# Layer embedding: the rounding of p, the splits of the first gate slabs, and the squares of the last gate slab, moved in the ScalarE and VectorE programs

## What is computed

```
f = swiglu_2(rmsnorm_2(h, g[4]), ffn_gate[i, 1], ffn_up[i, 1], ffn_down[i, 1])
h = h + MACARON * rmsnorm_2(f, g[5])
gate = jax.nn.sigmoid(rmsnorm_2(h, g[6]) @ w_ple_gate[i])
h = h + rmsnorm_2((p[i].astype(h.dtype) @ w_ple[i]) * gate, g[7])
```

## Time and profile before

| | us |
|---|---|
| median of 3 runs (1806.93 to 1814.6) | 1810.8 |
| the profiled execution itself | 1805.07 |
| its span, first to last instruction | 1803.4 |
| TensorE busy | 1713.6 (95%) |
| VectorE busy | 1180.2 (65%) |
| ScalarE busy | 897.7 (50%) |

### The profile page before, as it was taken

The page is one execution under the profiler, slowest core; times in us unless marked ns, Lnnn a source line. Parts: engine busy times, 40 slices in busy tenths (PEclk is TensorE's granted clock), DMA queues, the critical chain, the costliest instruction groups (busy, mean ns, idle before and its releaser), DMA issues.

```text
span 1803.4 us, 30032 instructions
## 1 busy us (share of the span) xinstructions
PE 1713.6 (95%) x11890; PEld 1595.1 (88%) x11890; DVE 1180.2 (65%) x1492; ACT 897.7 (50%) x1238; POOL 109.2 (6%) x161
## 2 busy tenths in 40 slices
PE   7988999999999999999999999988999998999996
PEld 4987999998899989999898899978999898899986
DVE  7988889867774456555675655565655675665556
ACT  4576533466543445343575543455433567543445
POOL 2110211100010000000020000000000003000000
PEclk9998999999999999999998999998999999999998
DMA  9983799946465554555441455534555442355550
GB/s 382 333 318 140 272 381 362 361 148 246 158 217 189 185 189 147 188 185 186 143 173 44 163 194 195 185 130 140 201 184 187 174 143 92 112 204 186 178 194 36
DMA packets 61924, 353.80 MB, mean 196 GB/s; under 512 B 6522, under 2 KB 9738, under 8 KB 27792
## 3 DMA queue, kind: packets, MB, share of 16 engines
q1 hardware_dynamic: 40064, 281.24, 42.6%
q0 software_dynamic: 18384, 66.66, 10.1%
q10 hardware_dynamic: 3392, 4.72, 0.8%
HBM read 349.45 MB, written 3.15 MB: 196 GB/s over the span
## 4 chain that ended last, share of the span: by engine, by line
PE 81%; DVE 9%; ACT 5%; issue 3%; DMA 2%; POOL 1%; DVEq 0%; ACTq 0%; POOLq 0%
PE bank L499 24%; PE bank L500 24%; PE bank L501 24%; DVE w_lo L1540 2%; ACT w_hi L1019 2%; PE bank L531 1%; PE bank L533 1%; PE bank L532 1%; PE bank L674 1%; DVE shared L2109 1%; DVE shared L1562 1%; DMA shared<-in_mods 1%; DVE x L2118 1%; DVE work L1924 1%; PE bank L557 1%
## 5 line engine op out<-in xcount | busy, mean ns | idle before, releaser
L499 PE MATMUL bank<-a_hi,w_hi 128*128 128x256 f32 x2648 | 757.2, 286 | 13.5 <-DVE a_lo L1613 3.8
L501 PE MATMUL bank<-a_hi,w_lo 128*128 128x256 f32 x2648 | 753.4, 285 | 0.0
L500 PE MATMUL bank<-a_lo,w_hi 128*128 128x256 f32 x2648 | 753.3, 284 | 0.0
L499 PEld LDWEIGHTS bank<-a_hi,w_hi 128*128 128x128 f32 x2648 | 512.4, 194 | 19.9 <-issue 10.4
L500 PEld LDWEIGHTS bank<-a_lo,w_hi 128*128 128x128 f32 x2648 | 512.4, 194 | 2.7 <-issue 0.5
L501 PEld LDWEIGHTS bank<-a_hi,w_lo 128*128 128x128 f32 x2648 | 512.0, 193 | 0.0
L1807 DVE TENSOR_TENSOR w_lo<-raw,w_hi 128x2048 fp32r<-128x2048 f32 x144 | 330.1, 2292 | 246.2 <-ACT w_hi L1160 246.2
L1160 ACT CAST w_hi<-raw 128x2048 fp32r<-128x2048 f32 x144 | 274.0, 1904 | 270.2 <-PE bank L501 270.2
L1540 DVE TENSOR_TENSOR w_lo<-raw,w_hi 128x2048 fp32r<-128x2048 f32 x122 | 279.5, 2294 | 135.9 <-ACT w_hi L1019 135.7
L1019 ACT CAST w_hi<-raw 128x2048 fp32r<-128x2048 f32 x122 | 231.6, 1907 | 90.8 <-PE bank L501 84.1
L499 PE MATMUL bank<-w_hi,hid_hi 128*128 128x512 f32 x548 | 216.2, 395 | 3.9 <-DVE hid_lo L2283 3.1
(11 more groups left out here) (251 smaller groups left out, 1904.3 us busy)
## 6 DMA issues: line engine op xcount, KB each, us to landing
raw<-in_stream SPq DMA_DIRECT2D x266, 1024.0 KB, 4.8
shared<-in_mods POOLq DMA_DIRECT2D x104, 512.0 KB, 6.8
grow<-in_rows POOLq DMA_DIRECT2D x12, 512.0 KB, 4.0
work<-in_mods POOLq DMA_DIRECT2D x8, 512.0 KB, 9.6
bias_rows<-work ACTq DMA_DIRECT2D x1, 2048.0 KB, 23.2
x<-in_x_t SPq DMA_DIRECT2D x1, 1024.0 KB, 6.0
x<-in_x_d ACTq DMA_DIRECT2D x1, 1024.0 KB, 7.6
work<-bias_rows ACTq DMA_DIRECT2D x1, 1024.0 KB, 8.6
```

Of the source, the lines that this page charges most:

```text
L499: pe.matmul(out, w_h, v_h, start=start, stop=False, skip_group_check=True)
L500: pe.matmul(out, w_h, v_l, start=False, stop=False, skip_group_check=True)
L501: return pe.matmul(out, w_l, v_h, start=False, stop=stop, skip_group_check=True)
```

## The change

Four moves, made for both layers of the second block. No instruction is added or removed, and TensorE's program is the same.

- ScalarE rounds p when the product of slab b+31 is done (`slab_done` at b+32), not b+32 (`slab_done` at b+33). Half 1 of `hid_hi` is last read by slab b+31.
- ScalarE rounds gate slabs b+34 and b+35 behind the roots of `post`. Before, one stood ahead of p and one between p and `post`.
- VectorE takes the low part of b+34 behind `post`. Before, it stood ahead of p.
- At the fourth gate slab ScalarE sums the squares ahead of the rounding of the next slab, not behind it. In layer 1 there is no next slab.

```diff
-            def ffn(i, b):
+            def ffn(i, b, embedded=None):
...
                 hidden_hi(j, j % 2, b + 3 * j - 1)
-                split_to(b + 3 * j + 5)
+                if embedded is not None:
+
+                    act.wait_ge(slab_done, b + 3 * FJ - 1)
+                    act.copy(hid_hi[:, 1], ptok[:, embedded]).then_inc(ph_ready, 1)
+                else:
+                    split_to(b + 3 * j + 5)
...
-                ffn(3 + 2 * l, bf)
-                act.wait_ge(slab_done, bf + 3 * FJ)
-                act.copy(hid_hi[:, 1], ptok[:, l]).then_inc(ph_ready, 1)
-                split_to(bf + 3 * FJ + 3)
+                ffn(3 + 2 * l, bf, l)
                 u = u2(l, 2)
                 post(u, 6 + 3 * l, bf + 3 * FJ - 1)
+                split_to(bf + 3 * FJ + 3)
                 turned_hi(u, gain2(l, 6))
...
-                    if i == 3:
+                    if i < 3:
+                        split_to(base2(l, M_PGATE) + i + 3)
+                        gated_squares(i)
+                    else:
                         warm_up()
-                    split_to(base2(l, M_PGATE) + i + 3)
-                    gated_squares(i)
+                        gated_squares(i)
+                        split_to(base2(l, M_PGATE) + i + 3)
...
         @block.vector
-                split_to(b + 3 * j + 5)
+                if i < 2 or i % 2 == 0:
+                    split_to(b + 3 * j + 5)
...
                 dve.tensor_tensor(hid_lo[:, 1], ptok[:, l], hid_hi[:, 1].bitcast(F32), ALU.subtract).then_inc(pl_ready, 1)
+                post(u2(l, 2), 6 + 3 * l, bf + 3 * FJ - 1, 0.5)
                 split_to(bf + 3 * FJ + 2)
-                post(u2(l, 2), 6 + 3 * l, bf + 3 * FJ - 1, 0.5)
```

## The result

| | median, us | runs | ratio to before, 95% interval |
|---|---|---|---|
| before | 1808.87 | 4 | |
| changed | 1789.46 (1788.47 to 1791.92) | 4 | 0.9894 [0.9873, 0.9916] |

The change saves 19.4 us (1.1%), between 15 and 23 by the interval. The forecast was 17.8 saved and 1793.0. The profiled execution took 1790.37, its span is 1788.7.

A forecast was written before the change was run, and what follows sets the result against it. The start of ScalarE's squares was taken to bound the stretch ahead of each layer's gate slabs. Twice 8.0 plus 1.8 gave 17.8 us, 1810.8 to 1793.0; likeliest range 1791 to 1797, with the first two rivals 1785 to 1802.

The forecast's parts named there:

- What bounds the stretch: Between the second network's last down product and the gate slabs, the start of ScalarE's squares sets the 15.8 us.
- The squares and the end of the residual: At each layer's second residual, the first square moves from 1195.53 to 1188.3 and x is complete 7.2 us earlier.
- The first gate slab: At the embedding of each layer, gate slabs start 8.0 us earlier, bounds 5.7 and 8.3, TensorE keeping full clock.
- the 16 transposes: On TensorE ahead of the gate slabs, priced at between 2.1 and 2.6 us from four in 0.66.
- The covers: Moved roundings fit ScalarE's 5.07 us idle time with 0.4 to spare; VectorE's low part is short by 0.1.
- The fourth square: The one thing that could hold `post`: ready at 1192.4, while VectorE asks for it at 1193.1.
- The squares of the fourth gate slab: At layer 0's fourth gate slab, putting squares ahead of the rounding saves 1.8 us, once; bounds 1.5 and 1.8.
- The clock: At layer 0's end, TensorE's idle time shrinks from 3.71 to 1.9 us; no difference from the clock was taken.
- both ends that the step named: At layer 0's end, either the clock holds, 2.0 us more gained, or falls later, costing up to 1 more.
- The rival by which it holds: The clock holds at layer 0's end because the pause is shorter: 19.8 us gained, 1791.0; chance 0.12.
- The squares' rival: Squares do not overlap the last down product: gain 5.0 us per layer, 11.8 in all, 1799.0; chance 0.12.
- The sum: Whole kernel: 16.0 + 1.8 = 17.8 us saved, median from 1810.8 to 1793.0; chance 0.68.

The follow-up runs named there:

- e4: Changed kernel, but p waits for the last down product and the fourth gate slab's squares stand as before; 0.9975 of the kernel before.
- e5: Changed kernel with one more wait: ScalarE's squares of each layer's second residual wait for the whole down product; 0.9935 of the kernel before.
- e1: Changed kernel without moving the fourth gate slab's squares ahead of the rounding; 0.9905 of the kernel before.
- e2: Kernel before with only the fourth gate slab's squares moved ahead of the rounding; 0.9985 of the kernel before.
- e3: Changed kernel with both slab roundings and the low part of b+34 ahead of the residual, fourth gate slab's squares as before; 0.9993 of the kernel before.
- a2: Changed kernel run again, unaltered, in a later comparison on its own chip; 0.9912 of the kernel before.
- a3: Changed kernel run again, unaltered, in another later comparison on its own chip; 0.9897 of the kernel before, median 1790.82 us.
- e6: Changed kernel with 19 instead of 12 unused-product calls ahead of turning x at layer 0's end and 6 behind; 0.9891 of the kernel before.
- e7: The kernel of e6 run once more; 0.9911 of the kernel before, median 1793.0 us.

## Why the prediction was right

- **What bounds the stretch.** The step said that the start of the squares sets it. e4 and e5 show it by size: 5.43 and 3.50 us of delay come back as 5.43 and 3.49.
- **The squares and the end of the residual.** Forecast 7.2 us earlier, measured 7.24 for the first square (12.88 to 5.64) and 7.22 for the end of x (20.44 to 13.22).
- **The first gate slab.** Forecast 8.0 with bounds of 5.7 and 8.3, measured 8.31 and 8.32, at the upper bound. 7.22 of them come with x and 1.09 behind it, where the clock had been at 0.50 in the kernel before and was at 1.00 in the changed one, as the forecast assumed. The gate slab follows x by 3.08 to 3.10 here and in e1, e4 and e5, all at full clock, and by 3.52 to 4.38 in the kernel before, e2 and e3, at half clock. The mis-sized term is the 16 transposes: priced at 2.1 to 2.6 from four in 0.66, they took 1.6, twice eight in 0.80 (1197.98 to 1198.78), since the end of the last transpose, which is in the 0.66, is paid once and not four times. TensorE was through at 1202.5 and waited some 0.2 for the second `a_lo`. So VectorE arrived last; I had TensorE last.
- **The covers.** ScalarE's two roundings fitted with 0.30 to spare (0.4 forecast). VectorE's low part was 0.23 short of its cover (0.1 forecast): `a_lo` was due at 1200.66 + 0.87 and started at 1201.76. The fourth square was no hindrance. No rounding behind them at the gate slabs waited for a transfer; slabs b+36 and b+37 were rounded in one run of 3.70 from 1207.59.
- **The squares of the fourth gate slab.** Forecast 1.8, measured 1.73 in the change and 1.81 alone (e2).
- **The clock.** I took no difference at the end of layer 0, and in the compared trace there was little: the clock fell at 1233.1, among the transposes and not ahead of them, and stayed low for 3.9 us of dense products (18 of them 0.21 apart, from 1236.03 to 1239.9), against 4.1 before. But this was partly luck. In the other traces with the short pause of 1.9 these products had 3.8 (a2), 5.9 (e2), 0 (e5) and 0 us (a3) at half clock; with the long pause they had 5.6 (e1), 3.3 (e3) and 3.4 (e4). So both ends that the step named came: the clock was back in time in a3 and e5, and it cost about 1 more in e2. The rival by which it holds is not out; its gain of 2.0 came as 1.7 in one of three traces of the changed kernel, and the times cannot tell it.
- **The squares' rival** (no overlap, 5.0 per layer) is out for the changed kernel: its squares ran in 0.58 to 0.60 beside TensorE's products, which kept their spacing of 0.23. The 0.60 is over the 0.58 that the prediction named as a sign for this rival, but by 0.02 only, and the third and fourth squares started when their pieces were done. e5, which forces that case, has 4.8 per layer.
- **The sum.** 17.8 forecast; 18.3 in the trace, 19.4, 17.1 and 17.7 in the three comparisons of times. The forecast median, 1793.0, was 3.5 above the measured one; 1.9 of this is the kernel before, whose median fell from the 1810.8 shown to 1808.87 with one run more.

## What to carry to other kernels

Where an engine runs its program in order, look for every instruction ahead of the urgent one that waits for the same event. Here p and a slab rounding both waited for the last down product and either alone held the squares: removing one of them gave 0.3 to 2.9 us per layer, removing both 8.3. Put the work that has a later deadline into the pause behind the urgent chain, and reckon the pause on the new times, row by row. The old trace had 5.07 us there, the new order left 4.0, and the 3.7 us of the two roundings fitted with 0.3 left. To compare two traces, count from a row just ahead of the change; the spans alone would have shown 14.7 of the 18.3 us. And take more than one trace before you say what the clock does: three traces of the same kernel gave 3.9, 3.8 and 0 us at half clock at one place.

## What the runs showed of the hardware

- Transposes of 128 x 128 in float32 followed each other by 0.10 us at full clock (eight in 0.80), though four of them stand in the timeline with 0.66.
- A table load written behind a semaphore wait need not wait: in e5 it ran at 1187.08, 4.8 us ahead of the warm-up that it serves, which did wait. The wait placed there cost nothing of the load's 1.28 us. Whether the compiler or the engine sets this order is not shown.
- The same program showed a different fall and return of the clock at one place: 30.4 and 37.2 us behind the first gate slab in the first trace, 28.3 and 31.7 in a3. It was worth 1.7 us.
- 13 more calls of no use kept the clock up and gained 1.7 us where it was kept (e6, e7), and those were gone 500 us later, in code that was the same. In a3 the same 1.7 us came without them and stayed.
